# The first attention: ScalarE's copy of the turned probabilities is issued ahead of the exponentials

## The reference

```python
q = rms_norm(q, q_norm_g)                     # 8 heads of 64, two kv heads
p_cmp = masked_softmax(s_cmp, cmp_end <= t)   # 31 compressed keys
o_cmp = einsum(p_cmp, vc)
# with 512 tokens there are 8 blocks of 64 and the top 16 are taken:
# every causal block, so the selected branch is causal attention
o_slc = causal_softmax(q, k_slc) @ v_slc
o_win = causal_softmax(q, k_win) @ v_win      # window 512 >= sequence
o = g[..., 0] * o_cmp + g[..., 1] * o_slc + g[..., 2] * o_win
```

## Time and profile before

| | us |
|---|---|
| runs of the kernel, median of 3 | 2647.99 |
| lowest and highest of them | 2644.48, 2649.97 |
| the profiled execution | 2645.53 |
| its span, first to last instruction | 2643.7 |
| TensorE busy in it | 2484.8 (94%) |
| VectorE, ScalarE, GpSimd busy | 1191.6, 919.7, 542.8 |
| mean granted TensorE clock | 0.964 |

### The profile page before, as it was taken

The page is one execution under the profiler, slowest core; times in us unless marked ns, Lnnn a source line. Parts: engine busy times, 40 slices in busy tenths (PEclk is TensorE's granted clock), DMA queues, the critical chain, the costliest instruction groups (busy, mean ns, idle before and its releaser), DMA issues.

```text
span 2643.7 us, 34280 instructions
## 1 busy us (share of the span) xinstructions
PE 2484.8 (94%) x14051; PEld 1981.5 (75%) x14051; DVE 1191.6 (45%) x1858; ACT 919.7 (35%) x1586; POOL 542.8 (21%) x391
## 2 busy tenths in 40 slices
PE   7887898899999989999999999999979999999998
PEld 5665666677778876678877888888856677878876
DVE  3735545453443336552266224223547634733433
ACT  3325543342221234452156221113335433632223
POOL 3003222140210222230013120013333210321023
PEclk8987898899999999999999999999889999999999
DMA  5230142244532311001300122123021023023232
GB/s 164 66 112 33 33 158 97 65 151 153 159 117 91 123 43 41 25 17 56 88 25 18 48 72 64 48 64 120 18 84 33 25 64 111 10 65 104 80 102 90
DMA packets 195741, 200.61 MB, mean 76 GB/s; under 512 B 15832, under 2 KB 189624, under 8 KB 195330
## 3 DMA queue, kind: packets, MB, share of 16 engines
q1 hardware_dynamic: 191106, 178.23, 21.5%
q10 hardware_dynamic: 4480, 20.19, 2.0%
HBM read 187.92 MB, written 10.49 MB: 75 GB/s over the span
## 4 chain that ended last, share of the span: by engine, by line
PE 83%; DVE 7%; ACT 4%; POOL 3%; issue 2%; DMA 1%; POOLq 0%; ACTq 0%; SPq 0%; DVEq 0%
PE PS L715 20%; PE PS L716 20%; PE PS L718 20%; PE PS L833 5%; PE PS L861 4%; PE PS L847 3%; DVE WL L1878 1%; ACT WH L1312 1%; PE PS L794 1%; PE PS L904 1%; PE PS L960 1%; POOL RB L2634 1%; PE PS L931 1%; PE PS L917 1%; PE PS L771 1%
## 5 line engine op out<-in xcount | busy, mean ns | idle before, releaser
L715 PE MATMUL PS<-HH,WH 128*128 128x512 f32 (+2 forms) x2096 | 776.5, 370 | 14.5 <-POOL HL L2783 8.1
L716 PE MATMUL PS<-HL,WH 128*128 128x512 f32 (+2 forms) x2096 | 743.8, 367 | 0.0
L718 PE MATMUL PS<-HH,WL 128*128 128x512 f32 (+2 forms) x2096 | 673.9, 365 | 0.0
L1878 DVE TENSOR_TENSOR WL<-WB,WH 128x2048 fp32r<-128x2048 f32 (+3 forms) x158 | 326.7, 2068 | 686.9 <-ACT WH L1312 679.2
L715 PEld LDWEIGHTS PS<-HH,WH 128*128 128x128 f32 (+1 forms) x2096 | 393.7, 188 | 124.8 <-issue 11.1
L716 PEld LDWEIGHTS PS<-HL,WH 128*128 128x128 f32 (+1 forms) x2096 | 393.8, 188 | 73.1 <-issue 2.9
L718 PEld LDWEIGHTS PS<-HH,WL 128*128 128x128 f32 (+1 forms) x2096 | 356.5, 188 | 46.2
L1312 ACT ACTIVATE WH<-WB 128x2048 fp32r<-128x2048 f32 (+3 forms) x158 | 265.1, 1678 | 345.1 <-PE PS L718 273.9
L2659 POOL TENSOR_SCALAR SA<-SA,ST 128x768 f32<-128x768 f32 (+4 forms) x80 | 141.4, 1768 | 536.7 <-DVE ST L1959 536.7
L2634 POOL TENSOR_TENSOR RB<-RB,SA 128x512 f32<-128x512 f32 (+2 forms) x65 | 88.1, 1356 | 389.8 <-ACT SA L1331 324.1
L1947 DVE TENSOR_REDUCE ST<-PS 128x1 f32<-128x768 f32 (+4 forms) x176 | 129.8, 738 | 74.4 <-PE PS L833 61.3
(11 more groups left out here) (367 smaller groups left out, 3675.2 us busy)
## 6 DMA issues: line engine op xcount, KB each, us to landing
WB<-in_w_in_dram SPq DMA_DIRECT2D x61, 1024.0 KB, 5.1
WB<-in_w_ff_dram SPq DMA_DIRECT2D x32, 1024.0 KB, 5.4
WB<-in_w_mod_dram SPq DMA_DIRECT2D x24, 1024.0 KB, 5.3
WB<-in_w_branch_dram SPq DMA_DIRECT2D x24, 512.0 KB, 3.4
WB<-in_w_o_dram SPq DMA_DIRECT2D x8, 1024.0 KB, 5.2
WB<-in_w_in_dram SPq DMA_DIRECT2D x14, 512.0 KB, 4.8
XTc<-xd ACTq DMA_DIRECT2D x2, 3072.0 KB, 10.6
WB<-in_cmp_w_dram SPq DMA_DIRECT2D x4, 1024.0 KB, 5.5
```

The lines of the kernel that those rows point to most:

```text
L715: pe.matmul(D[0:m, d + o:d + o + w], h, xh[:, o:o + w], start=first, stop=False)
L716: pe.matmul(D[0:m, d + o:d + o + w], h, xl[:, o:o + w], start=False, stop=False)
L718: t = pe.matmul(D[0:m, d + o:d + o + w], lo, xh[:, o:o + w], start=False, stop=last)
L1878: dve.tensor_tensor(b.of(WL[s % NH]), b.of(WB[b.n % NW]), b.of(WH[s % NH]).bitcast(F32), ALU.subtract).then_inc(*done("wl", s))
```

## The change

In ScalarE's `attend_pairs`, the block that copies the even unit of pair s-2 out of PSUM moves from behind the exponentials and fill A to the front of the step. Its two waits move with it: for the transposes of that unit in this step, and, from step 4 on, for the product of pair s-4, whose `PTn` it overwrites. The number of instructions stays the same, and the other engines' programs are untouched.

```diff
             def attend_pairs(A, after_put, fill):
                 fill = iter(fill)
                 for s in range(A.steps + 3):
+                    if 0 <= s - 2 < A.steps:
+                        u = 2 * s - 4
+                        parts = A.units[u]["parts"]
+                        w, e = parts[0][1], len(parts) * 128
+                        if s >= 4:
+                            act.wait_ge(*at("pv", A.name, s - 4))
+                        act.wait_ge(*at("tp", A.name, u))
+                        act.activation(A.PT[u % 4][0:w, 0:e], A.T(u)[0:w, 0:e], ACT.Copy).then_inc(*done("pt_a", A.name, u))
                     if s < A.steps:
                         for u in (2 * s, 2 * s + 1):
                             lo, w = A.units[u]["span"]
...
                             act.wait_ge(*at("mx", A.name, u))
                             act.activation(A.pb(u)[:, lo:w], A.S(u)[:, lo:w], ACT.Exp, bias=A.stat(u, 0), accum_out=A.stat(u, 1)).then_inc(*done("ex", A.name, u))
                     next(fill, None)
-                    if 0 <= s - 2 < A.steps:
-                        u = 2 * s - 4
-                        parts = A.units[u]["parts"]
-                        w, e = parts[0][1], len(parts) * 128
-                        if s >= 4:
-                            act.wait_ge(*at("pv", A.name, s - 4))
-                        act.wait_ge(*at("tp", A.name, u))
-                        act.activation(A.PT[u % 4][0:w, 0:e], A.T(u)[0:w, 0:e], ACT.Copy).then_inc(*done("pt_a", A.name, u))
                     if 0 <= s - 3 < A.steps:
```

## The result

| | before | after |
|---|---|---|
| median of the launches run together, us | 2649.6 (5 runs) | 2660.14 (5 runs) |
| lowest and highest | 2644.48, 2654.84 | 2658.18, 2662.69 |
| ratio, 95% interval | | 1.004 [1.0024, 1.0056] |
| profiled span | 2643.7 | 2658.3 |
| mean granted clock of the profiled execution | 0.964 | 0.959 |

The kernel became 10.5 us slower. The direction was the forecast's, the size twice the forecast's 5.2, and the time lies above the range (2658).

What follows compares the result with a forecast made beforehand. TensorE was taken to set the first attention's pace (busy 155.4 of 180.2 us). Delays through ScalarE's fill A, 1.10 + 0.49 + 0.97 + 0.76 + 0.57 + 1.65 - 0.32 = 5.2 us, gave 2653.2 us; range 2645.5 to 2658.

Steps and rivals of the forecast that it cites:

- The four waits for the copy: TensorE's transposes waiting 3.6 us for ScalarE's copy; removing them was valued at 0, bounds 0 and -3.6 us.
- the split of mk1's weights: ScalarE's split at 276.71 us goes behind the copy, delaying the scaling TensorE waits for; cost 0.49 us.
- mk1's square: Square in ScalarE's fill A, awaited by TensorE at 318.16 us, comes later behind the copy; cost 0.76 us.
- the copy of mv1: Copy out of PSUM whose slot TensorE awaits at 357.43 us comes later; cost 0.57 us.
- The weight split at 325.0: Another weight split in ScalarE's fill A, at 325.0 us, delayed behind the moved copy; cost 0.64 us.
- Am: First norm, step 3: root, spread matmuls and table load come later, delaying transposes at 228.85 us; cost 1.1 us.
- Mk0's square: Square at 293.74 us ends later behind the four-part copy, delaying TensorE's sum of columns; cost 0.97 us.
- The modulation's 0.35: The modulation's copy in ScalarE's fill A, at 363.1 us, delayed behind the moved copy; cost 0.35 us.
- clock: Rival: longer waits add one stretch of TensorE at 1.2 GHz, up to 5 us more, 2658 us; chance 0.15.
- Absorbed: Rival: delays vanish behind GpSimd or VectorE chains that end last anyway; 0 to 2 us over the median, 2649; chance 0.25.
- faster: Rival: the early copy frees TensorE and starts the step's chains sooner; 3.6 us off, 2644.4 us; chance 0.10.
- not what it says: Rival: the copy is held by its other wait, the product with V of pair s-4; no separate price or chance.

Runs made afterwards that it cites:

- e_spare: Kernel before with the copy moved first only in the 35 steps where no delay was forecast; ratio to before 1.0002, stage 183.6 us.
- e_only: Kernel before with the copy moved first only in the other 13 steps, where fill A feeds a late engine; ratio to before 1.0032, stage 191.7 us.
- e_one: Kernel before with the copy moved first in step 21 alone; ratio to before 1.0043, stage 180.1 us.
- e_late: Kernel before with the copy moved first in eight steps only, from 21 on; ratio to before 1.0026, stage 185.0 us.
- e_am: Kernel before with the copy moved first in steps 3 and 4 alone; ratio to before 1.0021, stage 187.1 us.
- e_delay: Kernel before, no copy moved, twelve small extra exponentials on ScalarE in each of steps 3 and 4; ratio to before 1.0035, stage 186.8 us.
- e_no34: The changed kernel, but with the copy in its old place in steps 3 and 4; ratio to before 1.0038, stage 187.8 us.
- r_after: The changed kernel built and run again, unaltered; 2661.69 us, ratio to before 1.0037, stage 191.7 us.
- e_mid: Kernel before with the copy moved only past fill A, so exponentials, copy, fill A; ratio to before 1.0017, stage 187.4 us.
- r_before: The kernel before built and run again, unaltered; 2651.31 us, ratio 0.9998, stage 183.4 us.
- w_before: Kernel before with 112 dummy matmuls on TensorE ahead of transposes that wait; ratio to before 1.004, stage 183.4 us.
- e_one_again: Repeat of the kernel before with the copy first in step 21 alone; median 2653.65 us, ratio to before 1.0011, stage 178.5 us.
- e_early: Kernel before with fill A put ahead of the exponentials and the copy last; ratio to before 1.0001, stage 180.9 us.

## Why the prediction was half right, and where it failed

**What held.** TensorE sets the pace; the order on ScalarE is the question, not its load. The four waits for the copy are worth nothing, because another releaser stands behind each: shown by e_spare (14.0 against 13.9 us). (One sentence of the prediction says three of the four; in the trace it is all four.) The steps without a term are free: e_spare. Lateness reaches TensorE through fill A at the places named: e_only holds the whole loss. The signs named came: the exponentials' wait went from 63.1 to 9.2 us, the table load came 2.5 us later, L771's wait for the squares went from 0.8 to 2.1 us; only the wait for GpSimd took over half of what was said, 1.8 of 3.6. Of the terms, measured against forecast, the split of mk1's weights was 0.55 in e_one (0.49), mk1's square 0.67 (0.76), the copy of mv1 0.55 (0.57) and that of mv0 0.54 (0.66). The weight split at 325.0 was 0.55 in the kernel after but 1.12 in e_late (0.64), so it isn't pinned down. Am was 1.42 (1.10). Mk0's square was 0.62 to 0.67, not 0.97: 0.11 less because the exponential after the 0.60 us copy starts 0.49 us after it, and 0.20 less because the exponential and the square, 292.85 and 293.74 before, stood 0.89 apart and now stand 0.69. The modulation's 0.35 was 0. All in all the plain delays came to 4.4 us in the kernel after; the sum had 5.2.

**The step that failed** is what the sum makes of these delays: "These delays add", to 5.2 us, with TensorE's clock put at nothing in it and kept as an alternative with a chance of 0.15. The same matmuls did not run at the same speed. Against before, TensorE spent 24 us more of the stage at 1.2 GHz (72 instead of 48), and that took 6.6 us, net of the 1.1 us less at the end of the stage, on top of the 4.4 of plain delay. The largest single carrier is the first term, am. Its chain was right link by link and 1.42 us long, but with it the stage grew by 3.7 to 6.9 us (e_am, against the two profiles of before); 4 us of extra ScalarE work in its place cost 3.4 to 6.6 (e_delay), and leaving it out saved 3.9 (e_no34 against r_after). It is not the only carrier: e_no34 and e_mid, without an early delay, have 61 us at 1.2 GHz, and r_before, with no change at all, has 55.

So the *clock* rival came true, but as an addition to the sum and not as an alternative to it. It was priced at 5 us for one added stretch; several stretches came, others went, and the net was 6.6. That the sum and the rival's price together, 5.2 + 5 us on 2649.6, give 2659.8, where 2660.1 was measured, is luck: the plain delays were smaller and the clock's share larger. Its mechanism was right in kind: in the steps without any idle time of TensorE (35 to 37, 42 to 44) the clock was never low, and filling waits with matmuls raised the mean clock from 0.87 to 0.96 (w_before). That agrees with what the Trainium skill, "TensorE: Matmul & The Clock Gate", section "HAM oscillation", says of bursts and gaps: each return to the throttled clock is paid again. But no single longer wait could be named as the cause of a stretch: the waits before the fall at 258.3 us were of 0.2 to 1.3 us, and steps 41 to 42 hold a wait of 1.31 us at the full clock. *Absorbed* and *faster* fell; *not what it says* too (no wait for the product with V ended a copy's idle time).

The rule of "Perfetto Trace Analysis", section "Optimization Strategy", in the Trainium skill, to make the blocking dependency start sooner, was followed by the change and gained nothing here; the next releaser and what is queued behind the new wait decided.

**What stays open.** Why low stretches come where they do: which wait, or which sum of waits, brings one on. The split of 4.4 and 6.6 us rests on single profiles, of which the kernel after has two that agree and the kernel before two that differ by 3.3 us. Why a program's executions fall into clumps 3 to 7 us apart (e_one_again), and whether that lies in the stage: e_one's profile is of a fast launch, while the median of its ten launches lies 11.7 us above that of before, as much as the whole change lost.

## What to carry to other kernels

Before moving an instruction ahead in an in-order queue, ask two things: what releases the waiting engine next once this wait is gone, and what is queued behind the wait that moves along. A copy that needs an engine's later result should stand behind work that needs only its earlier one. And where the stage mixes short waits with dense work, a delay may cost a multiple of its length through the clock; here 1.4 us of it, early in the stage, became 3.7 to 6.9. Take that as an addition to the sum, not as a rival. Cut the stage into intervals of the same work and compare length, idle time and clock one by one: that tells a plain wait from slower matmuls where the totals don't. And read a stage in several executions before trusting a difference of 3 us.

## What was unexpected of the hardware

- 4 us of extra ScalarE work in two steps (24 activations) cost 6.6 us of stage against the first profile, 3.4 against r_before, although no instruction of TensorE was touched.
- The same program's stage took 180.2 and 183.4 us, or 180.1 and 178.5, with clocks of 0.87 and 0.85, 0.88 and 0.89. With one copy moved and a stage no longer than before's, ten launches gave a ratio of 1.0043 and twelve others 1.0011; each set lay 16.5 us or more apart.
- Fewer waits did not mean a higher clock: e_early has 3 us less idle time than before and a clock of 0.84 instead of 0.87, and ends level.
